# Neighbourhood bias and mask added by TensorE in float32r, from tables split once

## The reference, cut to what matters

```python
# q, k, v: (B, S, H=8, Dh=64); rpb: (H, 15, 31)
# each block of 16 query columns sees kh=8 rows x 32 key columns, and 256 context keys
bias  = rpb[:, dr_idx[None, None, :, None], dc_idx[:, :, None, :]]
s_win = einsum('bcqhd,bkcjhd->bhcqkj', q_r, kb) * scale
s_win = where(col_ok, s_win + bias, -inf)
s_ctx = einsum('bcqhd,blhd->bhcql', q_r, k_ctx) * scale
p = softmax(concatenate([s_win, s_ctx], -1), -1)
o = p_win @ v_window + p_ctx @ v_ctx
```

## Time and profile before

| | |
|---|---|
| Median of 3 runs | 3448.81 us (3447.75 to 3458.78) |
| Profiled execution, own time | 3447.99 us |
| Its span | 3446.2 us, 38992 instructions |
| TensorE busy (matmul) | 2770.9 us, 80% |
| VectorE busy | 2074.6 us, 60% |
| ScalarE busy | 1221.7 us, 35% |
| GpSimd busy | 805.1 us, 23% |
| DMA | 848.12 MB, mean 246 GB/s |
| Mean granted TensorE clock | 0.894 of full |

### The profile page before, as it was taken

One profiled execution on the slowest core, in us unless ns is written; L12 is line 12 of the kernel. 1 busy time (PEld: TensorE's weight loads), 2 busy tenths in 40 slices (PEclk: granted clock), 3 DMA queues, 4 the chain that ended last, 5 costly groups with the idle time before them and its releaser, 6 DMA issues. The chain is left out here.

```text
span 3446.2 us, 38992 instructions
## 1 busy us (share of the span) xinstructions
PE 2770.9 (80%) x14561; PEld 2303.2 (67%) x14561; DVE 2074.6 (60%) x3720; ACT 1221.7 (35%) x2191; POOL 805.1 (23%) x724
## 2 busy tenths in 40 slices
PE   7999888995565556555556679979999999899998
PEld 5887677784455555554555667667888777778886
DVE  3224676487776864785455545356875465678753
ACT  2112433245555555555556541242111002422201
POOL 0002453124444444444444422001000000110000
PEclk9999999998767777777777779989999999999999
DMA  6999999779999999999999962202232231022222
GB/s 217 318 294 278 299 301 304 217 286 370 421 421 421 421 421 421 420 417 421 419 420 416 421 250 92 80 1 82 95 97 92 86 110 62 1 92 96 93 91 80
DMA packets 155057, 848.12 MB, mean 246 GB/s; under 512 B 15440, under 2 KB 15696, under 8 KB 88208
## 3 DMA queue, kind: packets, MB, share of 16 engines
q0 software_dynamic: 82624, 575.97, 41.4%
q1 hardware_dynamic: 72272, 269.99, 24.6%
HBM read 841.70 MB, written 136.31 MB: 284 GB/s over the span
## 5 line engine op out<-in xcount | busy, mean ns | idle before, releaser
L209 PE MATMUL PS<-AR_r,RHI 128*128 128x512 f32 (+2 forms) x1912 | 751.6, 393 | 30.6 <-DVE AR_r L1630 11.8
L211 PE MATMUL PS<-AR_r,RING_r 128*128 128x512 f32 (+2 forms) x1912 | 746.8, 391 | 0.0
L908 PE MATMUL PS<-IDN,HL 128*128 128x128 f32 x2688 | 480.7, 349 | 329.8 <-ACT HL L1434 329.8
L1820 DVE SCALAR_TENSOR_TENSOR AR<-AR 128x1024 f32<-128x1024 f32 x410 | 501.4, 1224 | 373.1 <-DMA AR<-peer_uv,XC 370.9
L908 PEld LDWEIGHTS PS<-IDN,HL 128*128 128x128 f32 x2688 | 415.4, 182 | 394.4 <-ACT HL L1434 389.0
L210 PE MATMUL PS<-AR_r,RHI 128*128 128x512 f32 (+1 forms) x1688 | 657.9, 390 | 0.0
L554 POOL DMA_INDIRECT AR<-peer_uv,XC x410 | 467.0, 1139 | 630.3 <-ACT HL L1434 315.6
L1612 DVE CAST RHI<-RING 128x1024 fp32r<-128x1024 f32 x256 | 178.7, 698 | 455.4 <-DMA RING<-in_wstream 452.4
L209 PEld LDWEIGHTS PS<-AR_r,RHI 128*128 128x128 f32 x1912 | 364.3, 191 | 110.5 <-issue 20.3
L211 PEld LDWEIGHTS PS<-AR_r,RING_r 128*128 128x128 f32 x1912 | 364.2, 190 | 74.0
L908 PE MATMUL PS<-IDN,AR 128*128 128x128 f32 x1408 | 259.4, 358 | 181.5 <-ACT AR L1434 181.5
(11 more groups left out here) (369 smaller groups left out, 3738.1 us busy)
## 6 DMA issues: line engine op xcount, KB each, us to landing
RING<-in_wstream SPq DMA_DIRECT2D x304, 512.0 KB
peer_uv<-in_peer_u SPq DMA_DIRECT2D x50, 1024.0 KB, 17.1
peer_uv<-in_peer_v SPq DMA_DIRECT2D x50, 1024.0 KB, 17.1
peer_uv<-in_peer_u POOLq DMA_DIRECT2D x14, 1024.0 KB, 20.4
peer_uv<-in_peer_v POOLq DMA_DIRECT2D x14, 1024.0 KB, 21.1
AR<-peer_uv,XC POOLq DMA_INDIRECT x410
XL<-in_xl SPq DMA_DIRECT2D x1, 2048.0 KB, 8.2
AR<-in_strips POOLq DMA_DIRECT2D x1, 2048.0 KB, 8.4
```

Source lines behind the costliest of these rows:

```text
L209: pe.matmul(out, sh, mh, start=start, stop=False)
L211: return pe.matmul(out, sl, mh, start=False, stop=stop)
L908: mm = pe.matmul(sum_bank(tt, k), scaled_row(n)[:, P * k:P * k + P], IDN[:], start=(j == 0 and k % 4 == 0), stop=(j == SLOTS - 1), is_tran ...
L1820: dve.scalar_tensor_tensor(u, u, 1.0, HT[:, n // SLOTS, :], ALU.mult, ALU.mult, accum_out=RAW[:, n:n + 1]).then_inc(dotted, 1)
```

## The change

The bias table `BT` (8 heads of 128x8x48, already in SBUF) is split once by GpSimd during the projections: eight float32r high parts into `XC` and `HC`, which are free once section `i` has been multiplied, a float32r copy of the mask beside them, and eight low parts over `BT` itself. TensorE then adds bias and mask to the scores by three float32r products for each head and step (high part, low part, mask) straight from the tables, in place of one float32 product from a tile. The tiles `NBM` are gone. GpSimd's loop in the attention only issues the copies of `peer_uv`, at the same steps as before. As `XC` now holds tables until the last scores, the level masks' load stands behind that loop and a wait for the last scores; the cast and the memset follow it as before.

```diff
-        NBM = [HCF[:, 256 * j:256 * j + 256] for j in range(4)]
+        BIAS_HEAD = NA_KH * BIAS_W
+        BIAS_HI = [over("XC", F32R, [P, NA_KH, BIAS_W], BIAS_HEAD * h) for h in range(5)] + [
+            over("HC", F32R, [P, NA_KH, BIAS_W], BIAS_HEAD * h) for h in range(3)]
+        BIAS_LO = over("AR", F32R, [P, NA_HEADS, NA_KH, BIAS_W], 27648)
+        NA_MASK = over("HC", F32R, [P, NCB, KB], 3 * BIAS_HEAD)
...
             barrier(pool, 1)
             pool.dma_start(BT, t["na_bias"]).then_inc(s_bt, 16)
+            pool.wait_ge(s_bt, 16)
+            pool.wait_ge(chunk_used, FIRST["i"] + 4)
+            for h in range(NA_HEADS):
+                steps.done(pool.tensor_copy(BIAS_HI[h][:], BT[:, h]))
+            steps.done(pool.tensor_copy(NA_MASK[:], par("na_mask").rearrange("p (b j) -> p b j", b=NCB)))
+            steps.wait()
+            for h in range(NA_HEADS):
+                ins = pool.tensor_tensor(BIAS_LO[:, h], BT[:, h], BIAS_HI[h][:].bitcast(F32), ALU.subtract)
+                ins.then_inc(na["bias"], 1)
             barrier(pool, 2)
+
+            for step in range(NA_STEPS):
+                if step >= 2:
+                    pool.wait_ge(na["s"], 2 * step - 3)
+                for _ in range(2 if step % 4 == 1 else 1):
+                    copy_rows(pool, next(late), uv_copied_late)
+            pool.wait_ge(na["s"], 2 * NA_STEPS)
             pool.dma_start(XCF, t["level_masks"]).then_inc(s_hm, 16)
-
-            pool.wait_ge(s_bt, 16)
-            for i in range(2 * NA_STEPS):
-                pair, b = divmod(i // 2, NCB)
-                h = 2 * pair + i % 2
-                off = QB * b - KC0[b]
-                if i >= 4:
-                    pool.wait_ge(na["s"], i - 3)
-                if i % 2 == 0:
-                    copy_rows(pool, next(late), uv_copied_late)
-                if i % 8 == 3:
-                    copy_rows(pool, next(late), uv_copied_late)
-                pool.tensor_tensor(NBM[i % 4].rearrange("p (k j) -> p k j", k=NA_KH), BT[:, h, :, QB - off:QB - off + KB],
-                                   par("na_mask")[:, KB * b:KB * b + KB].unsqueeze(1).to_broadcast([P, NA_KH, KB]),
-                                   ALU.add).then_inc(na["bias"], 1)
             pool.wait_ge(s_hm, 16)
             pool.tensor_copy(HM, XCF).then_inc(masks_ready, 1)
             pool.memset(MROWS[2], 0.0).then_inc(phase, 1)
...
             def na_scores(t):
                 pair, b = divmod(t, NCB)
-                pe.wait_ge(na["bias"], 2 * t + 2)
+                if b == 0:
+                    pe.wait_ge(na["bias"], 2 * pair + 2)
...
+                off = QB * b - KC0[b]
+                cols = slice(QB - off, QB - off + KB)
                 for x in range(2):
-                    pe.matmul(bank(2 * (t % 2) + x, 0, 256), IDN[:], NBM[(2 * t + x) % 4], start=False,
+                    h, to = 2 * pair + x, bank(2 * (t % 2) + x, 0, 256)
+                    pe.matmul(to, IDN_R[:], BIAS_HI[h][:, :, cols], start=False, stop=False)
+                    pe.matmul(to, IDN_R[:], BIAS_LO[:, h, :, cols], start=False, stop=False)
+                    pe.matmul(to, IDN_R[:], NA_MASK[:, b, :].unsqueeze(1).to_broadcast([P, NA_KH, KB]), start=False,
                               stop=True).then_inc(na["s"], 1)
```

## The result

Slower: 3462.22 us median (3452.98 to 3472.86, 20 runs) against 3448.62 us (20 runs of the kernel before beside it), +13.6 us, ratio 1.004, 95% interval 1.003 to 1.005. The forecast was 3451, range 3443 to 3459: the sign holds, and so does the first half of the mechanism (every engine waits for the masks' load behind GpSimd's copies). The size does not, and the median lies 3 us outside the range.

The account below looks back on a forecast made before the run. TensorE's steps and the DMA queues were taken to bound the attention; its 10.7 us gain is spent waiting. Barrier 3 +6.0 and behind it -3.3 give +2.7 on 3447.99: 3450.7, forecast 3451, range 3443 to 3459.

Parts of the forecast that it names:

- Products, start and attention's end: Attention: start 7.0 us earlier, steps 3.89 us instead of 4.17, so the attention's work ends 10.7 us sooner.
- the long first scaling: Attention's start: VectorE's first scaling pair, 3.29 us before, was taken at its median; if it stayed, 4.7 us gained, not 7.0.
- Splits in the projections: GpSimd's seventeen split instructions in the projections, 6 to 13 us, were to cost nothing, with some 10 us of cover.
- The masks' load behind the copies: End of attention: masks land at 394.5 (392.0 to 397.7), barrier 3 at 397.2 instead of 391.2: +6.0 us (+3.4 to +9.2).
- the 3.4 us that I credited to the first copy: Head of GpSimd's queue: with no load ahead, the first copy lands at 326.7 instead of 330.1.
- Behind barrier 3: GpSimd's queue empty, so chunk five takes 3 us, not 6.3; recurrence begins 18.1, not 21.4, us after: -3.3 (0 to -4.6).
- My check by DMA work: Round barrier 3: idle DMA engine time grows from 3.7 us to some 6 to 8, +3 to +4 for chunk six.
- Later stages: After the recurrence begins: cut off by chains that the attention stage only shifts; a shift in them got chance 0.03.
- Rival 1: Masks land 10.2 us after issue, at 381.5; barrier 3 at 384.2; -4.4 us, 3443.6; chance 0.14.
- Rival 2: End of GpSimd's queue: 19th copy, 20th and masks each take 6.6 us; masks land at 404.1; +12.3, 3460.3; chance 0.08.
- Rival 3: Bias products no faster, 0.25 us each; attention ends near 391; still 3450.7; chance inside the forecast's 0.72.
- rival 4: The attention's gain survives whole, masks and chunks both hidden: -10.7 us, 3437.3; chance 0.03.

Follow-up runs that it names:

- exp. 1: The changed kernel timed again with nothing altered: 3460.27 us, ratio 1.0033 to the kernel before.
- exp. 7: The changed kernel with 75 useless products ahead of TensorE's barrier 3, to keep its clock up: 3464.85 us, ratio 1.0039 to the kernel before.
- exp. 8: The changed kernel with 110 useless products ahead of TensorE's barrier 3: 3469.9 us, one run, with TensorE itself holding the barrier back.
- Experiment 3: The kernel before with only the masks' load moved behind the loop and a wait for the last scores: 3457.12 us, ratio 1.003.
- experiment 2: The changed kernel with the masks loaded at the head of the attention into idle weight slots: 3450.54 us, ratio 1.0008 to the kernel before.
- experiment 4: The changed kernel with the masks' load on the sync engine's queue, after the same wait: 3448.0 us, ratio 1.001 to the kernel before.
- experiment 5: The changed kernel with the masks' load ahead of the last four of GpSimd's 20 copies: 3449.51 us, ratio 0.9999 to the kernel before.

## Why the prediction was right or wrong

- **Products, start and attention's end: right, a little large.** I had 10.7 us from the start of the stage. Measured from barrier 2, the attention took 68.3 us instead of 77.3: 8.9. The start gave 7.0 as forecast, and the long first scaling did go with the tiles; a step fell by 0.14, not 0.28, as the first product and the switch to the values cost 0.1 each more than the pitch. That the pitch held was in part luck: the strided product of line 768 that I leaned on is float32, and shows nothing of float32r.
- **Splits in the projections: right.** They ran from 283.3 to 297.5, 14 us before GpSimd was released. Barrier 2 fell between 311.8 and 314.4 in the ten profiled kernels with the splits and between 310.2 and 313.9 in the four without, so a cost of a microsecond is not excluded.
- **The masks' load behind the copies: right in kind, low in size.** I had a landing at 394.5 with ends at 392.0 and 397.7, and barrier 3 at +6.0. Here is my sum beside four executions, in us measured from barrier 2, so that its own place drops out:

  | | forecast | changed | exp. 1 | exp. 7 | exp. 8 |
  |---|---|---|---|---|---|
  | first copy lands | 12.8 | 15.2 | 15.3 | 15.6 | 14.2 |
  | 18 intervals to the 19th | 61.0 | 61.5 | 62.5 | 61.9 | 61.2 |
  | 19th to 20th | 3.4 | 4.2 | 6.9 | 7.7 | 9.0 |
  | 20th to the masks | 3.4 | 2.5 | 2.5 | 2.4 | 2.4 |
  | masks land | 80.6 | 83.5 | 87.2 | 87.6 | 86.9 |
  | DMA share, 19th to 20th | | 0.62 | 0.47 | 0.37 | 0.35 |

  The mis-sized step is the end of the drain. I gave the 20th copy the steady 3.39 us, although my own row for it had 6.6 and I kept that for a bound; it took 4.2 to 9.0. The steady rate was right (3.40 to 3.47). The second miss is the 3.4 us that I credited to the first copy because no load stands ahead of it: it came 1.4 to 2.8 us later than that. Barrier 3 moved, measured from barrier 2, by +8.6, +12.2 and +12.7 in the three executions that the masks decided, where I had +6.0. Share times interval is 2.6 to 3.2 us in the four (an estimate from the table): about the same work, at a lower and lower share. Experiment 3 shows that the move alone makes most of the loss, experiments 2, 4 and 5 that undoing it in three ways removes it.
- **Behind barrier 3: wrong.** I credited 3.3 us, since GpSimd's queue would be empty, and so had chunk six 14.8 us after the barrier: 2 to the issue of chunk five's load, 3 for it, 9.8 from there to chunk six. Measured are 3.7, 4.0 and 10.6, together 18.3, and before it was 18.1. The issue was late by the fallen clock, 1.7 us (experiment 8), which I saw at the stage's start and didn't ask of its end. At full clock the terms are 1.9, 3.5 and 11.2: chunk five did come as forecast, but chunk six stands behind two copies of its own queue, and its load took 13 us with GpSimd's queue empty. My check by DMA work had 6 to 8 us of idle engine time; measured are 10.8 and 13.6.
- **Later stages.** I said that they are only shifted. They nearly are: in the profiled pair the second direction begins 6.9 us later, the first gather 6.2, the last gather 7.0; in experiment 1 it is 12.7, 14.6 and 17.3. Measured from barrier 2, the first gather is 8.1 and 16.6 us later, around the 13.6 of the medians. The profiled execution of the changed kernel was the one with the earliest landing, and its own +13.7 matches the medians by luck: the last 6 us of it came after the gathers, within the 14 us by which that part varies over all profiled executions, and the masks' landing gave only 8.6.
- **Rival 1 (the masks don't queue)** fell on GpSimd's queue and was true on the other. **Rival 2** (a late landing, deciding from 402, 3460) was the nearest to what happened, in the time and for one of its three transfers: the 20th copy did run slow at a share of 0.35 to 0.62. The 19th did not, and the masks came 2.5 us behind the 20th instead of 6.6. **Rival 3** was not met, **rival 4** fell: even with the masks out of the way (experiment 2, interval 0.9995 to 1.0021) at most 2 of the 9 us survive.

What stays open is why the last copy runs at a lower share in one execution than in another, and the exact split of the 13.6 us between landing and later stages.

## What to carry to other kernels

When a buffer is reused and a load must move, ask what stands ahead of it on the queue it is issued on, not only whether the engines are busy: here 1 MB took 24.8 us behind copies and 10.5 on another queue. Work won ahead of a barrier is worth nothing if the stage behind it waits for transfers that pass at the same rate whenever the barrier falls; look first at what the next stage waits for. Where a barrier leaves the DMA engines empty, don't credit the empty queue as a gain before you have asked what stands on the queue that the next stage waits for. And don't price the last transfer of a backlog at the backlog's steady rate: here it took 4.2 to 9.0 us against 3.4, and the stage waited for exactly that one and the one behind it.

## What the runs showed of the hardware

Two DMA queues with work for the same engines are served side by side: the same load at nearly the same moment landed after 10.5 us from the sync engine's queue and after 24.8 to 28.9 us from GpSimd's, with seven copies ahead. GpSimd's queue landed 1 MB copies every 3.40 to 3.47 us while it was full and took 4.2 to 9.0 us for the last, at a DMA share of 0.62 down to 0.35; a load issued ahead of a copy landed 3.1 us behind it. The float32r product of 256 columns keeps its 0.12 us pitch with strided and with broadcast operands. The two scalings took 0.88 us a pair beside no GpSimd work and up to 3.29 beside its tiles.
